# Attention's last four turned outputs get a PSUM bank each, and all their query tiles but the final one are turned one step earlier

## What is computed

```python
for i in range(DEPTH_2):
    ...
    out_a = chunk_gmlp(a_z, a_ws[i], a_bs[i])
    ...
    out_b = window_attn_latent(q_b, k_b, v_b, k_bc, v_bc, b_sink[i])
    ...
    o_c = diff_attn_latent(q_c, k_c, v_c, k_cc, v_cc, lam)
    out_c = (rms_norm(o_c, c_subln[i]) * (1 - lam_init)).reshape(b, l, C_WIDTH)
    x = x + g1 * (jnp.concatenate([out_a, out_b, out_c], axis=-1) @ w_out[i])
    x = x + g2 * conv_ffn(...)
    if not last:
        ...          # the same for ctx
```

## Time and profile before

| | us |
|---|---|
| median of three runs | 1784.94 |
| lowest, highest | 1782.21, 1786.73 |
| profiled execution | 1782.91 |
| its span, first to last instruction | 1781.1 |

### The profile page before, as it was taken

One profiled execution on the slowest core, in us unless ns is written; L12 is line 12 of the kernel. 1 busy time (PEld: TensorE's weight loads), 2 busy tenths in 40 slices (PEclk: granted clock), 3 DMA queues, 4 the chain that ended last, 5 costly groups with the idle time before them and its releaser, 6 DMA issues.

```text
span 1781.1 us, 29212 instructions
## 1 busy us (share of the span) xinstructions
PE 1702.5 (96%) x12118; PEld 1543.2 (87%) x12118; DVE 1236.3 (69%) x2077; ACT 868.6 (49%) x1295; POOL 201.8 (11%) x126
## 2 busy tenths in 40 slices
PE   6999999999999999999999999999999898899999
PEld 6999888898999999998767888788887887699999
DVE  2377479677777886477755798866778678458864
ACT  4422556447546665445655344323432445556653
POOL 5301560000000110100000111101110100041100
PEclk9999999999999999999989999999999899899999
DMA  7553545445345544421101334354334312035444
GB/s 270 220 206 143 213 163 200 194 163 204 142 168 180 178 178 162 160 94 55 65 1 48 119 128 156 136 189 151 141 137 169 124 72 95 1 137 186 177 165 142
DMA packets 41108, 259.75 MB, mean 146 GB/s; under 512 B 4368, under 2 KB 7568, under 8 KB 14480
## 3 DMA queue, kind: packets, MB, share of 16 engines
q1 hardware_dynamic: 40976, 257.88, 39.5%
HBM read 256.82 MB, written 1.05 MB: 145 GB/s over the span
## 4 chain that ended last, share of the span: by engine, by line
PE 82%; DVE 13%; ACT 3%; issue 1%; DMA 0%; POOL 0%; SPq 0%; DVEq 0%; ACTq 0%
PE acc_psum L197 23%; PE acc_psum L199 22%; PE acc_psum L198 22%; PE acc_psum L2427 3%; PE acc_psum L2380 2%; DVE w_low_sb L163 2%; PE acc_psum L2406 2%; PE acc_psum L1029 2%; PE acc_psum L238 1%; DVE mod_products L292 1%; PE acc_psum L373 1%; DVE ring_sb L292 1%; DVE u_filtered L1939 1%; DVE norm_sq_sb L676 1%; DVE norm_rt_sb L1676 0%
## 5 line engine op out<-in xcount | busy, mean ns | idle before, releaser
L197 PE MATMUL acc_psum<-h_high_sb,w_high_sb 128*128 128x256 f32 (+1 forms) x2176 | 669.7, 308 | 10.8 <-DVE h_low_sb L442 4.2
L198 PE MATMUL acc_psum<-h_low_sb,w_high_sb 128*128 128x256 f32 (+1 forms) x2176 | 662.1, 304 | 0.0
L199 PE MATMUL acc_psum<-h_high_sb,w_low_sb 128*128 128x256 f32 (+1 forms) x2176 | 661.8, 304 | 0.0
L152 ACT ACTIVATE w_high_sb<-ring_sb 128x1024 fp32r<-128x1024 f32 (+2 forms) x412 | 386.6, 988 | 409.2 <-PE acc_psum L199 289.2
L197 PEld LDWEIGHTS acc_psum<-h_high_sb,w_high_sb 128*128 128x128 f32 x2176 | 415.7, 191 | 38.6 <-issue 14.6
L163 DVE TENSOR_TENSOR w_low_sb<-ring_sb,w_high_sb 128x1024 fp32r<-128x1024 f32 (+1 forms) x356 | 387.4, 1130 | 85.6 <-ACT w_high_sb L152 75.2
L198 PEld LDWEIGHTS acc_psum<-h_low_sb,w_high_sb 128*128 128x128 f32 x2176 | 415.8, 191 | 17.6 <-issue 0.5
L199 PEld LDWEIGHTS acc_psum<-h_high_sb,w_low_sb 128*128 128x128 f32 x2176 | 415.3, 191 | 16.8
L163 POOL TENSOR_TENSOR w_low_sb<-ring_sb,w_high_sb 128x1024 fp32r<-128x1024 f32 x56 | 136.7, 2465 | 755.0 <-ACT w_high_sb L152 755.0
L1939 DVE SCALAR_TENSOR_TENSOR u_filtered<-acc_psum,par_sb,u_filtered 128x255 f32<-128x255 f32 (+2 forms) x264 | 150.7, 571 | 75.3 <-ACT u_filtered L2076 58.4
L197 PE MATMUL acc_psum<-u_high,w_high_sb 128*128 128x256 f32 (+1 forms) x528 | 170.6, 323 | 9.1 <-DVE w_low_sb L163 9.1
(11 more groups left out here) (303 smaller groups left out, 2008.4 us busy)
## 6 DMA issues: line engine op xcount, KB each, us to landing
ring_sb<-in_w_in SPq DMA_DIRECT2D x68, 1024.0 KB, 6.7
ring_sb<-in_w_up SPq DMA_DIRECT2D x66, 1024.0 KB, 4.8
ring_sb<-in_w_down SPq DMA_DIRECT2D x48, 704.0 KB, 4.0
ring_sb<-in_w_ada SPq DMA_DIRECT2D x24, 1024.0 KB, 4.8
ring_sb<-in_w_ada_rows SPq DMA_DIRECT2D x24, 1024.0 KB, 4.8
ring_sb<-in_w_out SPq DMA_DIRECT2D x12, 1024.0 KB, 4.7
ring_sb<-in_w_br_hg SPq DMA_DIRECT2D x4, 1024.0 KB, 6.9
ring_sb<-in_w_br_ml SPq DMA_DIRECT2D x4, 1024.0 KB, 4.9
```

Of the source, the lines that this page charges most:

```text
L152: self.nc.scalar.activation(self.high[:, g % 2, piece], self.ring[:, c % RING, piece], ACT.Copy)\
L197: nc.tensor.matmul(out, sh, mh, start=start, stop=False)
L198: nc.tensor.matmul(out, sh, ml, start=False, stop=False)
L199: return nc.tensor.matmul(out, sl, mh, start=False, stop=stop)
```

## The change

The four last entries of SIDE get the banks 0, 1, 4 and 5 (`side_bank`). Behind the value products of the tail's second-last step TensorE turns for each of them all query tiles but the final one (three in layer 0, one in layer 1). In the last step it turns the final tile of each and raises `su`. Entries 6 and 7 wait, at their early part, for the reads of entries 4 and 5, as before; entries 8 and 9 wait for the last exponentials, which read the scores' banks. The entry with j = 2 waits for `b_done` of as many tiles as it turns. The readers take the new bank numbers, and the projection's first use of banks 4 and 5 now waits for `su_read`.

```diff
+    def side_bank(n):
+        return n % 2 if n < 8 else n - 4
...
-            def side_use(n):
+            def side_use(n, tokens):
 
                 what, j = SIDE[n]
-                bank = n % 2
-                if n < 2:
-
-                    pe.wait_ge(*act_read.at(NS))
-                else:
-
-                    pe.wait_ge(*su_read.at(n - 1))
+                bank = side_bank(n)
+                if tokens.start == 0:
+                    if n < 2:
+
+                        pe.wait_ge(*act_read.at(NS))
+                    elif n < 8:
+
+                        pe.wait_ge(*su_read.at(n - 1))
+                    else:
+
+                        pe.wait_ge(*exr.at(rank(U)))
...
-                        pe.wait_ge(*b_done.at(NQ))
+                        pe.wait_ge(*b_done.at(tokens.stop))
...
-                    for t in range(NQ):
+                    for t in tokens:
                         mm = nc.tensor.transpose(psum[:, bank, t * P:(t + 1) * P], src[:, t, c:c + P], ident)
-                mm.then_inc(*su.one())
+                if tokens.stop == NQ:
+                    mm.then_inc(*su.one())
...
             for st in TAIL:
                 first_part(st)
                 second_part(st)
+                if st == TAIL[-2]:
+                    for n in range(6, len(SIDE)):
+                        side_use(n, range(0, NQ - 1))
                 for n in side_at(st):
-                    side_use(n)
+                    side_use(n, range(NQ) if n < 6 else range(NQ - 1, NQ))
...
-    reads = {b: [exr.at(0)] for b in (2, 3, 4, 5)} | {b: [su_read.at(0)] for b in (0, 1)}
+    reads = {b: [exr.at(0)] for b in (2, 3)} | {b: [su_read.at(0)] for b in (4, 5, 0, 1)}
```

More of the change, by code:

```diff
@@ L2665, in side_read @@
                     act.wait_ge(*su.at(n + 1))
-                    nc.scalar.activation(H[0][:, j, 0:T], psum[:, n % 2, 0:T], ACT.Copy).then_inc(*cat_high.one())
+                    nc.scalar.activation(H[0][:, j, 0:T], psum[:, side_bank(n), 0:T], ACT.Copy).then_inc(*cat_high.one())
             cat_high = sig("cat_high")
@@ L2903, in side_read @@
                     dve.wait_ge(*cat_high.at(n - 1))
-                    nc.vector.tensor_tensor(H[1][:, j, 0:T], psum[:, n % 2, 0:T], H[0][:, j, 0:T].bitcast(F32), ALU.subtract)\
+                    nc.vector.tensor_tensor(H[1][:, j, 0:T], psum[:, side_bank(n), 0:T], H[0][:, j, 0:T].bitcast(F32), ALU.subtract)\
                         .then_inc(*su_read.one())
```

## The result

The changed kernel takes 1771.93 us (median of four runs, 1770.33 to 1773.72); the kernel before, on the same chip, 1784.18. The ratio is 0.9939, with a 95% interval from 0.9921 to 0.9958: 10.9 us less, where 5.1 were forecast and 1776.8 us was the lower end of the range. The profiled execution took 1770.33 us.

A forecast was written before the change was run, and what follows sets the result against it. TensorE, busy 96% of the span and 82% of the chain, was taken to bound the kernel. Gains of 3.5 us (layer 0) and 1.6 (layer 1), 5.1 together, off 1784.94 gave 1779.8 us, range 1776.8 to 1782.8.

The forecast's parts named there:

- the clock term: Both ends of attention: gain chosen by whether TensorE's granted clock falls; 3.5 us taken in layer 0, 1.6 in layer 1.
- The places and the order of the work: Both attention ends: early transposes fill TensorE's wait, four follow the release, projection starts 0.45 to 0.9 us after it.
- The clock term, layer 0: End of layer 0's attention: gain 3.5 us, the middle of 2.5 (old end at full clock) and 4.5.
- The clock term, layer 1: End of layer 1's attention: gain 1.6 us, between 1.0 (clock falls as profiled) and 2.6 (stays up).
- The case that I gave 0.15: Both attention ends: full clock throughout, gain 4.5 + 2.6 = 7.1 us, run 1777.8 us; chance 0.15.
- I let the gain through to the end: Behind both attention ends: everything starts from TensorE, so the whole 5.1 us gain reaches the run's end.
- The slower case: Output projections of both layers: a long half-clock stretch makes the run 6.2 us slower, 1791.1 us; chance 0.05.
- the forecast's own range: Both attention ends, main case: gain 3.5 to 6.6 us around 5.1, run 1778.3 to 1781.4 us; chance 0.60.
- the second case: Both attention ends at full clock: gain 7.1 us, run 1777.8 us; chance 0.15.
- the third: Both attention ends: half clock in spite of the shorter wait, gain 2.6 us, run 1782.3 us; chance 0.12.

The follow-up runs named there:

- the filled kernel: The kernel before with unused identity transposes in TensorE's wait at attention's end (12 in layer 0, 4 in layer 1): 0.9978 against the kernel before.
- the filled norm above: The changed kernel with unused transposes both around the norm spread behind layer 1's projection and in both tails' waits: 1764.7 us, 0.9902 against the kernel before.
- experiments 3 and 6: 3: the change in one layer alone, 0.9971 (layer 0), 0.9975 (layer 1); 6: the changed kernel with unused transposes in norm, tails, both: 0.9941, 0.9908, 0.9902.
- experiment 1: Unedited repeats: the kernel before against itself 1.0015; the changed kernel against the kernel before 0.9963 and 0.9964.
- 5 and 6: 5: the changed kernel with 15 unused transposes in layer 1's attention, 0.9966; 6: with unused transposes in norm, tails, both: 0.9941, 0.9908, 0.9902.

## Why the prediction was wrong

The step that failed is the clock term: 5.1 us were forecast for the two ends, and they gave 6.7 to 7.3, because in both layers half clock stood at the old end in every profile and at the new one in none. That alone would have ended near 1778, inside the range. The rest of the first measurement is spread that the forecast took too small.

- **The places and the order of the work: right.** Early transposes directly behind the last values, no wait of the projection for VectorE's reads, none for POOL (1548.25 + 4.75, in time for the second half of its unit), none for cond_rows. The starts came at the lower end of what was given: 0.41 us behind the release in both layers. Of the old distance at full clock I had worked out 3.0 us and a gain of 2.5 in layer 0; the filled kernel has 3.05, and from it to the changed kernel the end shrinks by 2.7.
- **The clock term, layer 0: mis-sized.** I took 3.5, the middle between 2.5 (no half clock before) and 4.5. The half clock before is no matter of chance: it came in all five profiles in which layer 0's end was unchanged or had one part only (mean clock 0.71 to 0.84), and in none of eight with both parts (1.00), nor in the one with the wait filled. By the starts of the instructions the gain is 11.06 or 11.66 less 7.08, so 4.0 to 4.6 us.
- **The clock term, layer 1: the wrong case.** I took 1.6, near the fall, because 1.2 us of wait stayed. It stayed (1.17), and the clock did not fall in any of eight profiles with the edit in layer 1, while it fell in all five that had there nothing or one part of it (0.73 to 0.76). The gain is 2.7 us. The case that I gave 0.15, full clock through both ends (7.1 us), is what happened there: 6.7 to 7.3. What the Trainium skill says of the default level (TensorE: Matmul & The Clock Gate, "The HAM clock gate") agrees with this (1.00 in the second and fourth window) better than my choice did; the cycling around banks of its "A second HAM failure mode: psum-queue depth-cycling" showed no effect at these places. Elsewhere the trace does not bear the first out: in the earlier trace rows and in the filled norm above the clock was at 0.50 and 0.51 for 12.00 and 3.40 us with TensorE busy all the time, and there the measurement decides.
- **"I let the gain through to the end": wrong by 1.0 us.** Layer 1's edit costs 1.0 in the norm behind, by where the half clock falls (experiments 3 and 6).
- **What was left out: the spread of one kernel.** Ends less norm make 5.7 to 6.3 us, and twelve and eleven runs measured 6.4 and 6.6. The first comparison measured 10.9, four runs on each side. Most of the surplus lies with the kernel before: 1784.18 us in the first comparison, 1780.6 to 1781.4 in the later ones (34, 35 and 17 runs), while the changed kernel took 1771.93 first and 1772.3 and 1773.6 later (not all on one chip). The first pair of profiles contains 3.8 and 2.5 us from half-clock stretches in the attention. Layer 0's short stretch came without the edit as well (experiment 1), and layer 1's long one came with the edit in place (5 and 6); layer 1's 51.7 us came in no profile without the edit (54.1, 54.2 or 52.4), so part of the 2.5 may be the change's after all. That the surplus of the first ratio came from there is likely, but only argued; two later ratios at 0.9963 and 0.9964 do not repeat it, though their intervals overlap with that of the first (0.9921 to 0.9958). I had taken the spread from three runs (4.5 us, "about 1 us" for a median); 35 runs span 12.5 us. The range should have been wider by that alone.
- **The slower case** needed a long half-clock stretch in the projection. None came in any of the eight profiles of either layer with both parts.
- **The ends of the ranges.** The 6.6 us as the upper end of the forecast's own range has no working, and the whole range allows 1.0 us below the second case but 0.5 above the third. Neither changes what is said here.

## What to carry to other kernels

A wait of TensorE has two prices: its own length, and the products at half clock behind it. Look in the windows' clock column at what stands around each such wait, and take more than one profile: a fall that comes at the same wait each time (five of five here) belongs to that wait, one that comes and goes is no edit's gain. Then move real work into the wait, or try filling it with work that nobody reads if there is a free bank, and look whether the clock followed. Where one kernel's runs spread over 0.7%, neither one profile nor three runs can carry a difference of 0.3%: time the kernel against itself first.

## What the runs showed of the hardware

- Unused transposes made the kernel faster: 28 in each tail are worth 9 to 10 us, at about 0.12 us each (18 of them took 2.13 us at full clock). They did not keep the clock up in one of the two profiles with a filled norm: 0.51 over 3.40 us of busy TensorE.
- At the ends of attention a wait of 1.17 us did not bring the clock down in any of eight profiles. A wait of 1.7 us did in every one, and so did waits of 0.95 and 1.30 us (layer 0) or 1.39 and 0.82 us (layer 1) one behind the other; 1.26 and 0.72 us (the filled kernel, layer 1) did not.
- Stretches of the same code (but for a few transposes at their end) took 69.3, 73.1 or 76.6 us (layer 0's attention) and 51.7, 52.4 or 54.4 us (layer 1's), in steps that go with the mean clock of the stretch (0.95, 0.91, 0.87 and 0.93, 0.90, 0.87). The same kernel gives more than one of them, so where the clock falls there depends on something besides the program's text; what stays open.
